# The last stage of a decoder layer: a place for every chunk's rows, loads moved ahead of it, four additions on TensorE

## The reference, cut to what matters

```python
# x: (1, 1024, 1024), after the mixer's residual;  h = rms_norm(x, norm2_w)
y = grouped_expert_ffn(tokens, expert_ids, w_gate, w_up, w_down)    # (n, 2, D)
out = jnp.einsum('nk,nkd->nd', weights.astype(y.dtype), y)
x = x + out.reshape(bsz, t_len, d)
return rms_norm(x, final_norm_w)
```

## Time and profile before

| | us |
|---|---|
| median of 3 runs | 2226.93 (2224.96 to 2229.48) |
| the profiled execution, its device time | 2230.12 |
| its span, first to last instruction | 2228.3 |
| TensorE busy in the span | 1998.3 (90%) |
| VectorE busy in the span | 1325.1 (59%) |
| ScalarE busy in the span | 940.3 (42%) |
| granted TensorE clock, mean over the span | 0.954 |

### The profile page before, as it was taken

One profiled execution on the slowest core, in us unless ns is written; L12 is line 12 of the kernel. 1 busy time (PEld: TensorE's weight loads), 2 busy tenths in 40 slices (PEclk: granted clock), 3 DMA queues, 4 the chain that ended last, 5 costly groups with the idle time before them and its releaser, 6 DMA issues. The chain is left out here.

```text
span 2228.3 us, 25317 instructions
## 1 busy us (share of the span) xinstructions
PE 1998.3 (90%) x10102; PEld 1664.4 (75%) x10103; DVE 1325.1 (59%) x1426; ACT 940.3 (42%) x1012; POOL 367.8 (17%) x209
## 2 busy tenths in 40 slices
PE   4999999999989999989997999985599999999970
PEld 3778888888978777777775788775488888888860
DVE  4740000576115777767873665565599999999945
ACT  5120101112114433444442334242578888888842
POOL 3213323243410000000000100011122222222200
PEclk9999999999989999999998999997699999999995
DMA  4133222123235543654543754451799999999947
GB/s 154 59 144 102 98 91 95 59 93 132 76 101 144 144 136 115 158 140 144 148 133 126 259 210 185 150 220 48 255 370 381 387 387 387 390 385 385 388 181 264
DMA packets 218988, 435.85 MB, mean 196 GB/s; under 512 B 30770, under 2 KB 153666, under 8 KB 191234
## 3 DMA queue, kind: packets, MB, share of 16 engines
q1 hardware_dynamic: 185698, 354.63, 45.9%
q10 hardware_dynamic: 21152, 54.53, 6.7%
q0 software_dynamic: 12032, 25.22, 3.0%
HBM read 369.67 MB, written 81.43 MB: 202 GB/s over the span
## 5 line engine op out<-in xcount | busy, mean ns | idle before, releaser
L583 DVE TENSOR_SCALAR tap<-u,taps 128x1024 f32<-128x1024 f32 x16 | 20.1, 1298 | 294.0 <-ACT u L541 294.0
L613 PE MATMUL ps<-h_hi,w_hi 128*128 128x512 f32 x576 | 178.4, 391 | 4.8 <-PEq L58 4.8
L613 PE MATMUL ps<-h_lo,w_hi 128*128 128x512 f32 x576 | 178.4, 391 | 0.0
L613 PE MATMUL ps<-h_hi,w_lo 128*128 128x512 f32 x576 | 178.3, 391 | 0.0
L2296 DVE TENSOR_TENSOR gu_lo<-gate_raw,gu_hi 128x2048 fp32r<-128x2048 f32 x64 | 146.7, 2293 | 48.1 <-ACT gu_hi L2243 48.1
L1247 PE MATMUL psum<-h_hi,l_hi 128*128 128x512 f32 x384 | 160.5, 418 | 7.3 <-PEq L58 7.3
L1247 PE MATMUL psum<-h_lo,l_hi 128*128 128x512 f32 x384 | 161.0, 419 | 0.0
L1247 PE MATMUL psum<-h_hi,l_lo 128*128 128x512 f32 x384 | 160.6, 418 | 0.0
L2296 DVE TENSOR_TENSOR gu_lo<-up_raw,gu_hi 128x2048 fp32r<-128x2048 f32 x64 | 146.3, 2288 | 13.4 <-ACT gu_hi L2243 13.4
L2301 DVE TENSOR_TENSOR dn_lo<-dn_raw,dn_hi 128x2048 fp32r<-128x2048 f32 x62 | 142.0, 2292 | 16.0 <-ACT dn_hi L2253 13.0
L551 ACT ACTIVATE out<-ps 128x2048 f32<-128x2048 f32 x14 | 26.4, 1883 | 271.1 <-PE ps L613 202.1
(11 more groups left out here) (352 smaller groups left out, 5024.3 us busy)
## 6 DMA issues: line engine op xcount, KB each, us to landing
gate_raw<-moe SPq DMA_DIRECT2D x66, 1024.0 KB, 8.8
up_raw<-moe SPq DMA_DIRECT2D x64, 1024.0 KB, 8.4
dn_raw<-moe SPq DMA_DIRECT2D x62, 1024.0 KB, 7.8
w_raw<-w_in SPq DMA_DIRECT2D x26, 1024.0 KB, 6.7
dn_raw<-w_br SPq DMA_DIRECT2D x16, 1024.0 KB, 7.5
l_raw<-w_gates ACTq DMA_DIRECT2D x24, 512.0 KB, 4.9
s_gates<-l_out ACTq DMA_DIRECT2D x48, 256.0 KB, 4.0
gate<-s_gates SPq DMA_DIRECT2D x16, 768.0 KB, 5.4
```

The source lines that it names most:

```text
L583: ins = nc.vector.tensor_scalar(tap[:, a, :], u[b][:, a, 0:T], taps[b][:, a, 0:1], None, ALU.mult)
L613: ins = nc.tensor.matmul(ps[b][:, a * T + half * 512:a * T + half * 512 + 512], w[:, k, a * P:(a + 1) * P], h[:, k, half * 512:half * 512 ...
```

## The change

In `experts_first_slabs`, SP loads the `s_x2` rows of the last three chunks too, into `dn_raw` (free once the second last expert's down pieces are split: `dn_ready`), and the final norm's weights. Then it waits for the last multiplication (`dn_used`) and for both scatter semaphores, loads `todo`, and begins the `s_pairs` loads of chunks 0 to 3 into the four `gu_raw` buffers. Each of the eight loads has a semaphore that outlives the stage. In `experts_further_slabs`, SP begins the loads of chunks 4 to 7 into four new buffers before it reads `todo`; if the loop is entered, POOL first waits for all eight loads, and loads them once more behind the loop. In `finish` no load is left, every chunk has its own place, TensorE adds the two rows of chunks 1, 3, 4 and 6 (identity times each row, summed in PSUM), DVE then adds `x2` from PSUM, DVE's order is add(c) and then the scaling of c-1, and the stores are issued by SP, which waits for all of them at the end.

```diff
+            sp.wait_ge(dn_ready, DN * LAST)
+            for n, tail in enumerate(x2_tail):
+                c = len(x2_kept) + n
+                sp.dma_start(tail, dr["x2"][c * CH:(c + 1) * CH, :]).then_inc(x2_in, 16)
+            sp.dma_start(final_w, io["final_norm_w"].unsqueeze(0).to_broadcast([P, D])).then_inc(x2_in, 16)
+            sp.wait_ge(dn_used, DN * N_EXPERTS)
+            for b in range(2):
+                sp.wait_ge(scattered[b], 16 * N_EXPERTS // 2)
+            sp.dma_start(todo[:], dr["work"].rearrange("(o n) w -> o (n w)", o=1)).then_inc(todo_in, 16)
+            for c in range(GU):
+                sp.dma_start(pairs[c], pair_rows(dr, c)).then_inc(pairs_in[c], 16)
+            sp.wait_ge(x2_in, 16 * (NCH + 1))
...
+def pair_rows(dr, c):
+    return dr["pairs"].rearrange("(a t) d -> t a d", a=2)[c * CH:(c + 1) * CH]
...
 # experts_further_slabs, SP:
+            for c in range(GU, NCH):
+                sp.dma_start(pairs[c], pair_rows(dr, c)).then_inc(pairs_in[c], 16)
             sp.sem_inc(slab_done, 1)
-            sp.dma_start(todo[:], dr["work"].rearrange("(o n) w -> o (n w)", o=1)).then_inc(todo_in, 16)
 # POOL, inside the test on todo's first word, ahead of and behind the loop:
+            def first_load_past():
+                for c in range(NCH):
+                    pool.wait_ge(pairs_in[c], 16)
+            def load_again():
+                for c in range(NCH):
+                    pool.dma_start(pairs[c], pair_rows(dr, c)).then_inc(loaded_again, 16)
+                pool.wait_ge(loaded_again, 16 * NCH)
+            slabs(pool, body, first_load_past, load_again)
...
+def finish(nc, out, ident, x2, final_w, todo_in, pairs, pairs_in):
+    ON_PE = (1, 3, 4, 6)
+        sem = semaphores(nc, ctx, [todo_in] + pairs_in)
+        both = [ctx.enter_context(nc.psum_tensor(f"both{b}", [P, D], F32)) for b in range(len(ON_PE))]
 # SP:
+                sp.wait_ge(y_ready, c + 1)
+                sp.dma_start(out[c * CH:(c + 1) * CH, :], pairs[c][:, 1, :]).then_inc(stored, 16)
+            sp.wait_ge(stored, 16 * NCH)
+        @block.tensor
+        def _(pe):
+            for n, c in enumerate(ON_PE):
+                pe.wait_ge(pairs_in[c], 16)
+                for half in range(2):
+                    hs = slice(half * 512, half * 512 + 512)
+                    for a in range(2):
+                        ins = nc.tensor.matmul(both[n][:, hs], ident[:], pairs[c][:, a, hs], start=a == 0, stop=a == 1)
+                ins.then_inc(both_ready, 1)
 # DVE:
+            def add(c):
+                if c in ON_PE:
+                    n = ON_PE.index(c)
+                    dve.wait_ge(both_ready, n + 1)
+                    two = both[n][:]
+                else:
+                    dve.wait_ge(pairs_in[c], 16)
+                    own.link(nc.vector.tensor_tensor(pairs[c][:, 0, :], pairs[c][:, 0, :], pairs[c][:, 1, :], ALU.add))
+                    two = pairs[c][:, 0, :]
+                nc.vector.tensor_tensor(x2[c], x2[c], two, ALU.add).then_inc(sum_ready, 1)
+            def scaled(c):
+                dve.wait_ge(rstd_ready, c + 1)
+                nc.vector.scalar_tensor_tensor(pairs[c][:, 1, :], x2[c], stat[:, c, 1:2], final_w, ALU.mult, ALU.mult)\
+                    .then_inc(y_ready, 1)
             for c in range(NCH):
-                if c + 1 < NCH:
-                    add(c + 1)
+                add(c)
+                if c >= 1:
+                    scaled(c - 1)
+            scaled(NCH - 1)
```

More of the change, by code:

```diff
@@ L44, with semaphores @@
 IN_W = _at
-def semaphores(nc, ctx):
-    made = []
+def semaphores(nc, ctx, older=()):
+    made = list(older)
     def clear():
@@ L2089, in _, with experts_first_slabs @@
             nc.tensor.matmul(cnt_ps, ones[:], cnt[:], start=True, stop=True).then_inc(cnt_ready, 1)
-def experts_first_slabs(nc, io, dr, ident, dn_raw, gate_raw, x2_kept):
+def experts_first_slabs(nc, io, dr, ident, dn_raw, gu_raw, x2_kept, x2_tail, final_w, todo, todo_in, pairs, pairs_in):
     LAST = N_EXPERTS - 1
@@ L2381, in _, with experts_further_slabs @@
             down(LAST)
-def experts_further_slabs(nc, io, dr, ident):
+def pair_rows(dr, c):
+    return dr["pairs"].rearrange("(a t) d -> t a d", a=2)[c * CH:(c + 1) * CH]
+def experts_further_slabs(nc, io, dr, ident, todo, todo_in, pairs, pairs_in):
     FK = FF // P
@@ L2391, in experts_further_slabs @@
         wg, wu, wdn = sb("xwg", [P, KT, FF]), sb("xwu", [P, KT, FF]), sb("xwd", [P, FK, D])
-        todo = sb("todo", [1, 2 * 16], I32)
         rec = sb("xrec", [P, 4], U32)
@@ L2418, in experts_further_slabs, with slabs @@
         slab_done = sem("slab_done")
+        loaded_again = sem("loaded_again")
         passed = sem("passed")
         block = ctx.enter_context(nc.Block())
-        def slabs(eng, body):
+        def slabs(eng, body, ahead=None, behind=None):
             eng.wait_ge(todo_in, 16)
@@ L2426, in slabs @@
             with eng.If(any_place > 0):
+                if ahead:
+                    ahead()
                 with eng.Fori(0, N_EXTRA) as n:
@@ L2431, in slabs @@
                         body(n, place, expert)
+                if behind:
+                    behind()
         @block.sync
         def _(sp):
+            for c in range(GU, NCH):
+                sp.dma_start(pairs[c], pair_rows(dr, c)).then_inc(pairs_in[c], 16)
             sp.sem_inc(slab_done, 1)
-            sp.dma_start(todo[:], dr["work"].rearrange("(o n) w -> o (n w)", o=1)).then_inc(todo_in, 16)
             def body(n, place, expert):
@@ L2514, in _ @@
             slabs(pe, body)
-def finish(nc, io, dr, out, x2_kept):
+def finish(nc, out, ident, x2, final_w, todo_in, pairs, pairs_in):
+    ON_PE = (1, 3, 4, 6)
     with ExitStack() as ctx:
         sb = lambda name, shape, dt=F32: ctx.enter_context(nc.sbuf_tensor(name, shape, dt))
-        sem = semaphores(nc, ctx)
-        NB = 4
-        rows = [sb(f"rows{b}", [P, 3, D]) for b in range(NB)]
+        sem = semaphores(nc, ctx, [todo_in] + pairs_in)
         sq = sb("fsq", [P, D])
-        fw = sb("fw", [P, D])
         stat = sb("fstat", [P, NCH, 2])
         cst = sb("fcst", [P, 1])
-        loaded = [sem(f"loaded{b}") for b in range(NB)]
-        fw_in = sem("fw_in")
+        both = [ctx.enter_context(nc.psum_tensor(f"both{b}", [P, D], F32)) for b in range(len(ON_PE))]
         c_ready = sem("c_ready")
+        both_ready = sem("both_ready")
         sum_ready = sem("sum_ready")
@@ L2533, in finish @@
         y_ready = sem("y_ready")
-        stored = [sem(f"stored{b}") for b in range(NB)]
+        stored = sem("stored")
         dve_own = sem("dve_own")
@@ L2555, in _ @@
             nc.vector.memset(cst[:], EPS).then_inc(c_ready, 1)
-            dve.wait_ge(fw_in, 16)
             def add(c):
[L2559 to L2566, removed]
-            for c in range(NCH):
-                if c + 1 < NCH:
-                    add(c + 1)
[L2570 to L2573, removed]
+                if c in ON_PE:
[11 more added lines that the diff above has]
+                    .then_inc(y_ready, 1)
+            for c in range(NCH):
+                add(c)
+                if c >= 1:
+                    scaled(c - 1)
+            scaled(NCH - 1)
         @block.scalar
@@ L2580, in _ @@
             for c in range(NCH):
-                b = c % NB
                 act.wait_ge(sum_ready, c + 1)
-                own.link(nc.scalar.activation(sq[:], rows[b][:, 0, :], ACT.Square, accum_out=stat[:, c, 0:1]))
+                own.link(nc.scalar.activation(sq[:], x2[c], ACT.Square, accum_out=stat[:, c, 0:1]))
                 own.link(nc.scalar.activation(stat[:, c, 0:1], stat[:, c, 0:1], ACT.Ln, scale=1.0 / D, bias=cst[:]))
                 nc.scalar.activation(stat[:, c, 1:2], stat[:, c, 0:1], ACT.Exp, scale=-0.5).then_inc(rstd_ready, 1)
[L2586 to L2589, removed]
 def build(nc, io, out):
@@ L2623, in build @@
         dn_raw, gate_raw = many(DN, "dn_raw", [P, DK, D]), many(AHEAD, "gate_raw", [P, GK, FF])
+        pairs_in = [ctx.enter_context(nc.semaphore(f"pairs_in{c}")) for c in range(NCH)]
+        todo_in = ctx.enter_context(nc.semaphore("todo_in"))
         merge_and_route(nc, io, dr, ident, dn_raw, gate_raw)
         x2_kept = many(KEPT, "x2_kept", [P, D])
-        experts_first_slabs(nc, io, dr, ident, dn_raw, gate_raw, x2_kept)
-        experts_further_slabs(nc, io, dr, ident)
-        finish(nc, io, dr, out, x2_kept)
+        x2_tail = [dn_raw[n // DK][:, n % DK, :] for n in range(NCH - KEPT)]
+        final_w = dn_raw[DN - 1][:, DK - 1, :]
+        gu_raw = gate_raw + many(GU - AHEAD, "up_raw", [P, GK, FF])
+        todo = ctx.enter_context(nc.sbuf_tensor("todo", [1, 2 * 16], I32, side="right"))
+        pairs = [t[:].rearrange("p k f -> p (k f)").rearrange("p (a d) -> p a d", a=2) for t in gu_raw]
+        experts_first_slabs(nc, io, dr, ident, dn_raw, gu_raw, x2_kept, x2_tail, final_w, todo, todo_in, pairs, pairs_in)
```

(3 more changed lines are left out.)

4 lines of the change are left out of this document (removed).

## The result

The changed kernel takes 2206.25 us (median of 4 runs, 2204.45 to 2210.03) against 2226.86 (median of 4); ratio 0.9904, 95% interval 0.9888 to 0.992. Forecast were 2206.7 us and faster. The profiled execution took 2204.45, its span 2202.7.

What follows compares the result with a forecast made beforehand. No resource was full: loads waiting for stores, plus dead time before the last stage, bound the tail. Stage start 2176.2 plus DVE's path gave span end 2208.1, 20.2 less; from median 2226.93, forecast 2206.7 us, range 2203 to 2213.

Steps and rivals of the forecast that it cites:

- the ring: Last stage: four buffers where a load waits for the store four chunks before; chain shows load waits of 8.54 and 8.46.
- the dead time: Ahead of the last stage, 2166.0 to 2175.4: no sizable transfer runs; most of it is POOL's drain, 5.28 us.
- x2 rows and weights at nothing: Experts' stage: loading 2.1 MB early costs nothing while DMA engines are nearly idle; without that cover, 5.5 us.
- First four loads hidden under POOL's drain: Behind the last scatter: SP issues todo and four loads by 2168.4, hidden by POOL's drain until 2171.4.
- The last stage 0.8 later: Further slabs' stage: four issues take 2.0 us instead of one issue and a 1.2 us wait, so finish starts at 2176.2.
- Landing times: Pair-row loads at 384 GB/s: chunk 0 lands at 2170.7, chunk 3 at 2178.9, chunk 7 at 2189.8.
- DVE's work: Last stage: DVE has 24.4 us of work left against 29.14; its path ends at 2204.6, the span at 2208.1.
- The stall before chunk 1: Start of the last stage: DVE waits 3.2 us for TensorE's addition, done at 2181.8 after starting at 1.2 GHz.
- TensorE at 1.2 GHz throughout: Rival, last stage: TensorE's clock never rises, its chunks come late, time 2214.1 us; chance 0.08.
- A stage change longer under traffic: Rival, before the last stage: drain or code fetch waits for loads, up to 7.5 us later, 2214.2 us; chance 0.11.
- The transfers binding: Rival, last stage: 12.6 MB at 278 GB/s last until 2213.3, time 2212.6 us; chance 0.06.
- Signs: Trace, if right: loads issued from 2166, last stage near 2176, one DVE wait of about 3 us; wrong: experts' stage ending after 2161.

Runs made afterwards that it cites:

- e4: Kernel before the change with eight buffers instead of four in the last stage, nothing else: 2223.33 us, ratio 0.9971, tail 54.7 us.
- e1: Changed kernel with all additions on DVE again and TensorE idle in the last stage: 2213.57 us, ratio 0.9926, tail 42.8 us.
- e3: Changed kernel with all eight pair-row loads issued in the last stage and no addition on TensorE: 2216.21 us, ratio 0.994, tail 47.2 us.
- e12: Changed kernel run once more with no edit: 2209.99 us, ratio 0.9912 to the kernel before, tail 41.5 us.
- e5: Changed kernel with norm weights and x2 rows of chunks 5 to 7 loaded behind the last scatter: 2214.1 us, ratio 0.9913, tail 47.4 us.
- e8: Changed kernel without POOL's own wait for the last scatter; SP still waits: 2206.29 us, ratio 0.9883.
- e9: Changed kernel without POOL's wait for the last scatter, and with loads of chunks 4 to 7 issued in the last stage: 2207.03 us, ratio 0.9896.
- e10: e9 with ACT's table load and POOL's clearing in the passed-over part, and chunks 3, 5, 6, 7 on TensorE: 2205.54 us, ratio 0.9889.
- e2: Changed kernel with all eight pair-row loads issued at the start of the last stage: 2214.98 us, ratio 0.9945, tail 48.7 us.
- e7: Changed kernel with chunks 3, 5, 6, 7 on TensorE instead of 1, 3, 4, 6: 2207.75 us, ratio 0.9888, tail 38.2 us.
- e6: Changed kernel with unread identity products on TensorE ahead of the last stage to keep its clock up: 2209.54 us, ratio 0.9906, tail 39.4 us.

## Why the prediction was right, point by point

*Transfers were not the bound of the kernel before, the ring and the dead time were.* Shown for the ring by e4 (DVE's waits for loads 11.0 to 3.8) and for the dead time by e1 against e3; but once the ring is gone the transfers bind (e4, 407 GB/s), which the prediction does not say. Following the tails, 62.2 to 54.7 is the ring (e4); 54.7 to 47.2 everything that e3 has besides, which is the x2 rows and weights moved ahead, stores from SP and `todo` fetched earlier (no run parts them; e3's waits above say how much each could be); 47.2 to 42.8 the early loads; 42.8 to 40.4 or 41.5 TensorE. The parts are not a sum of independent terms: TensorE's is nothing with the loads late. By medians on one chip the steps e4 to e3 (7.1) and before to e4 (5.9) are clear of noise, e3 to e1 (2.6) is not.

*x2 rows and weights at nothing.* Right: from the weighing to the drain's start it is 4.2 us, 4.3 before, and the medians gain 20.6 and 21.9 (e12) where the tails gain 21.8 and 20.7, so no cost ahead of the tail shows. The forecast price without the cover, 5.5 us, was met in size by e5 (from 9.8 to 15.3) and missed in kind: I had it as traffic, it is SP standing in an issue in front of a barrier.

*First four loads hidden under POOL's drain.* Right: SP leaves at 2165.1, the drain ends at 2167.6. The fourth issue took 0.87 and not 0.45, which the cover hid.

*The last stage 0.8 later.* 0.4 (9.8 behind the drain's start for 9.4). The four issues took 1.9 for 2.0, and SP read `todo` 2.0 behind its entry for 1.2, as priced; from that read to the next stage it then took 1.7 for 1.9, which no run explains. What the step overlooked is that they could have taken 3.7 or 7.3 us (e8, e5): they were priced from rows of an emptier queue, and the place was nearly full.

*Landing times.* Too early by about a microsecond: chunk 0 was put 4.6 behind the drain's start and landed 5.4 behind it (issued 2162.5, 5.2 later); chunk 6 at 20.8, seen at 22.2 (TensorE took it up at 2184.5). The rate was 400 to 418 GB/s for 384, so what was late is the first landing. The cover hid it in the change; in e9 and e10 the landing times decide.

*DVE's work.* Forecast 31.9 (2176.2 to 2208.1) from the stage's start to the end of the span, measured 30.6 and 31.7. The stall before chunk 1, forecast 3.2, is 2.58 and 3.67, and 4.05 and 4.10 in e8 and e5. From its end to the last scaling's end 22.04 for 22.6, and DVE's busy time 23.81 for 24.4.

*The rivals.* TensorE at 1.2 GHz throughout: no, the granted clock was 0.64 over 2172 to 2176 and 1.00 after, until its work was done. A stage change longer under traffic: no, the drain is 5.278 with and without, and the further slabs' stage 2.67 and 2.65 (e9, e2). The transfers binding: no, 400 to 418 GB/s while loads run, and no DVE wait on one; but in e4 and e10 they do bind.

*Signs.* The times of the trace that the prediction names (loads from 2166, the stage near 2176) came 3.8 to 4.1 earlier, with the whole tail. An experts' stage that ends later than 2161, named as a sign of being wrong, is none: with code that is the same or nearly so up to there, the weighing ends anywhere between 2156.1 and 2166.9.

*Code fetch.* The prediction took from the Trainium skill ("Runtime: NRT & Kernel Launch", section on instruction fetch mechanics) that a taken branch out of the window held forces a fetch by DMA. Such a fetch cost nothing visible in those 2.67 us under traffic; whether one took place is not shown.

The forecast's 20.2 for the tail against 21.8 measured, 20.7 with the repeat, is the sum of these small terms: 0.4 from the stage's start, 0.6 from the stall and 0.6 from DVE's work in the first profile, while the stall of the repeat was 0.5 over the forecast. That the median came within 0.5 us is partly luck, since the medians of the changed kernel in its two sets of runs were 2206.25 and 2209.99.

## What to carry to other kernels

A ring in which a load waits for a store shows in the chain of waits as loads and stores in turn beside DMA engines that are not full; give each piece its own place, and count what it is worth by changing the number of buffers alone. When loads are moved ahead of a barrier, add up what is pending in the issuing engine's queue: an issue that finds it full holds the engine, and a barrier behind it holds all of them (e5). Help from an engine whose clock is low should get a piece that is wanted late, not the next one.

## What the runs showed of the hardware that was not expected

SP's issue of a 1 MB load mostly takes 0.36 to 0.53 us while up to an estimated 5.3 MB are pending ahead of it; the fourth issue in a row takes 0.63 to 0.90 in all of them, the change and e1 to e12, and why stays open. With 5.4 MB or more ahead of it an issue takes 1.05 to 2.66 us (the last in e2), and 2.95 for one load of 0.5 MB in e4. POOL's drain behind an indirect DMA took 5.278 us behind its wait, in every kernel with that wait, and 6.49 from its own start without it, overlapping the scatter; a wait for the landing in front of it only adds. What the drain does in that time stays open. TensorE's first eight records in the last stage took 5.06 and 6.15 us in the change and its repeat, and between 5.27 and 6.58 in e2, e5, e7, e8, e9 and e10, all after 13.5 to 23.4 us of idleness, and 3.67 when it had been kept busy (e6). The landing of the same first load varies as well: 5.2 us behind its issue in both profiles of the change, 6.2 in e6, 6.7 in e2.
